# First two slabs behind a layer norm multiplied by input quarters, in a two-layer hybrid block on one core

## What is computed

```python
for l in range(DEPTH):                 # DEPTH = 2
    ...                                # proj = x @ w_in; main mixer; memory attention
    mixed = jnp.concatenate([main, mem_out], axis=-1) @ w_out[l]
    x = layer_norm(DEEPNORM_ALPHA * x + mixed, ln_g[l, 0], ln_b[l, 0])
    ffn = peer_ffn(x, peer_wq[l], peer_subkeys[l], peer_u[l], peer_v[l])
    x = layer_norm(DEEPNORM_ALPHA * x + ffn, ln_g[l, 1], ln_b[l, 1])
```

## Time and profile before

| | us |
|---|---|
| median of 3 runs | 3369.53 |
| lowest and highest of them | 3367.92 and 3376.97 |
| profiled execution | 3374.42 |
| its span, first to last instruction | 3372.6 |
| TensorE busy in it | 3321.4 |
| VectorE, ScalarE busy | 2779.2, 1925.3 |

### The profile page before, as it was taken

One profiled execution on the slowest core, in us unless ns is written; L12 is line 12 of the kernel. 1 busy time (PEld: TensorE's weight loads), 2 busy tenths in 40 slices (PEclk: granted clock), 3 DMA queues, 4 the chain that ended last, 5 costly groups with the idle time before them and its releaser, 6 DMA issues.

```text
span 3372.6 us, 51763 instructions
## 1 busy us (share of the span) xinstructions
PE 3321.4 (98%) x19516; PEld 2994.8 (89%) x19516; DVE 2779.2 (82%) x3848; ACT 1925.3 (57%) x3368; POOL 487.6 (14%) x264
## 2 busy tenths in 40 slices
PE   8999999999999999999999999999999999999998
PEld 7888879999999988887887887999999998888887
DVE  4664669998999978888986756999899988888897
ACT  5555545555666655555555545555666665555555
POOL 0000000011222211222310000011122221212330
PEclk9999999999999999999999999999999999999999
DMA  7554345797999989999984344578799988999995
GB/s 256 176 182 142 113 157 189 260 348 276 366 364 361 358 317 357 357 360 364 367 322 149 119 154 148 202 288 336 286 365 359 363 337 338 358 361 367 378 379 216
DMA packets 169074, 969.04 MB, mean 287 GB/s; under 512 B 18897, under 2 KB 52689, under 8 KB 55377
## 3 DMA queue, kind: packets, MB, share of 16 engines
q1 hardware_dynamic: 132048, 698.61, 55.6%
q0 software_dynamic: 36864, 268.45, 21.0%
HBM read 951.26 MB, written 15.73 MB: 287 GB/s over the span
## 4 chain that ended last, share of the span: by engine, by line
PE 91%; DVE 5%; DMA 2%; ACT 1%; issue 1%; SPq 0%; DVEq 0%; ACTq 0%
PE ps L943 90%; DVE wl L1577 1%; DMA raw<-in_v 1%; DMA arena<-in_v,idx 1%; PE ps L1133 1%; ACT wh L536 0%; DVE arena L1736 0%; DVE xx L1595 0%; DVE arena L1912 0%; DMA raw<-in_w 0%; DVE arena L1702 0%; DMA raw<-in_u 0%; ACT arena L595 0%; DVE arena L1680 0%; DVE arena L1683 0%
## 5 line engine op out<-in xcount | busy, mean ns | idle before, releaser
L1577 DVE TENSOR_TENSOR wl<-raw,wh 128x1024 fp32r<-128x1024 f32 x1264 | 1527.4, 1221 | 475.8 <-ACT wh L536 472.0
L943 PE MATMUL ps<-xx,wh 128*128 128x384 f32 (+1 forms) x5504 | 1710.2, 372 | 16.5 <-DVE wl L1577 11.5
L536 ACT ACTIVATE wh<-raw 128x1024 fp32r<-128x1024 f32 x1264 | 1334.9, 1057 | 618.9 <-PE ps L943 550.6
L943 PE MATMUL ps<-xx,wl 128*128 128x192 f32 (+1 forms) x5504 | 1422.0, 258 | 0.0
L943 PE MATMUL ps<-wh,act 128*128 128x512 f32 x3584 | 1190.7, 390 | 7.4 <-DVE act L1600 7.3
L943 PEld LDWEIGHTS ps<-xx,wh 128*128 128x128 f32 x5504 | 1034.4, 188 | 79.5 <-DVE wl L1577 11.8
L943 PEld LDWEIGHTS ps<-xx,wl 128*128 128x128 f32 x5504 | 1049.6, 191 | 0.5
L943 PE MATMUL ps<-wl,act 128*128 128x512 f32 x2304 | 897.1, 389 | 0.0
L943 PEld LDWEIGHTS ps<-wh,act 128*128 128x128 f32 x3584 | 673.4, 188 | 149.9 <-DVE wl L1577 6.7
L943 PEld LDWEIGHTS ps<-wl,act 128*128 128x128 f32 x2304 | 432.9, 188 | 89.6
L1548 POOL DMA_INDIRECT arena<-in_v,idx x128 | 272.4, 2128 | 834.1 <-DVE arena L1912 814.4
(11 more groups left out here) (213 smaller groups left out, 1698.3 us busy)
## 6 DMA issues: line engine op xcount, KB each, us to landing
raw<-in_u SPq DMA_DIRECT2D x256, 1024.0 KB
raw<-in_v SPq DMA_DIRECT2D x256, 1024.0 KB
raw<-in_w SPq DMA_DIRECT2D x119, 1024.0 KB
h_scratch<-hring SPq DMA_DIRECT2D x128, 96.0 KB
hring<-h_scratch SPq DMA_DIRECT2D x128, 96.0 KB
arena<-in_memT SPq DMA_DIRECT2D x4, 512.0 KB, 6.6
arena<-in_xT SPq DMA_DIRECT2D x4, 512.0 KB, 7.6
arena<-in_urows,idx POOLq DMA_INDIRECT x128
```

The lines of the kernel that those rows point to most:

```text
L536: nc.scalar.activation(wh[:, j, :], raw_piece(p), ACT.Copy).then_inc(hi_ready, 1)
L943: return nc.tensor.matmul(out, lhs, rhs, start=start, stop=stop, **kw)
L1577: v.tensor_tensor(wl[:, j, :], raw_piece(p), wh[:, j, :].bitcast(F32), ALU.subtract).then_inc(lo_ready, 1)
```

## The change

It touches the four norms and what stands directly before and behind them.

1. The first two slabs behind norms 0, 1 and 2 are multiplied together by a new function, `first_pair`: quarter 0 for slab 0 and slab 1, then quarter 1 for both, and so on. Quarters 0 to 2 are turned first; quarter 3 is turned after slab 0's share of quarter 0.
2. So the first halves of both slabs are needed before their second halves. `half_of` gives the new order: pieces p0, p0+1 are the first halves of slabs 0 and 1, p0+2 and p0+3 the second halves. The same order holds for the last two slabs of the N and V stages. In these, ScalarE makes the high part of each activation right behind one piece, not two, with a wait on `piece_used` of its own.
3. The norm centres four parts of 512 columns and goes by quarters: `turn(n, q)` turns banks q and 4 + q. Both engines finish quarter 0 (turned, high, low) before they start on quarter 1. Four pieces of the next stage are split inside the norm (AHEAD is gone, RING takes its place).
4. The side copy of slab 0 waits for one piece more (`split_by`), and the scores of heads 0 and 1 both stand in slab 2.

The core of the diff:

```diff
+def half_of(p):
+    for p0 in PAIRED_FIRST + PAIRED_LAST:
+        if p0 <= p < p0 + RING:
+            return p0 // 2 + (p - p0) % 2, (p - p0) // 2
+    return p // 2, p % 2
+
+def split_by(n):
+    return 2 * n + 2 + (2 * n in PAIRED_FIRST + PAIRED_LAST)
...
@@ SyncE
-                sp.wait_ge(lo_ready, 2 * (n - RAW_SLABS) + 2)
+                sp.wait_ge(lo_ready, split_by(n - RAW_SLABS))
@@ ScalarE, take_side
-            act.wait_ge(piece_used, k * 2 + (p0 + 2))
+            act.wait_ge(piece_used, split_by(p0 // 2) if k == 0 else k * 2 + (p0 + 2))
...
@@ ScalarE, norm
+            for q in range(3):
+                centred(q)
+            turned(0)
+            if n < 3:
+                high(0)
+            centred(3)
+            turned(1)
+            if n < 3:
+                high(1)
+            turned(2)
+            if n < 3:
+                high(2)
+                hi(p_next + 2, 2)
+                hi(p_next + 3, 3)
+            turned(3)
+            if n < 3:
+                high(3)
...
@@ ScalarE, v_trip
+                paired = i == S_EXP // 2 - 1
                 for s in range(2):
-                    for e in range(2):
-                        hi(i * RING + (v0 + 2 * s + e), 2 * s + e)
+                    for j in (s,) if paired else (2 * s, 2 * s + 1):
+                        hi(i * RING + v0 + j, j)
+                    if paired:
+                        act.wait_ge(piece_used, i * RING + v0 - 2 + 2 * s)
...
+                for j in (2, 3) if paired else ():
+                    hi(i * RING + v0 + j, j)
@@ TensorE
+        def first_pair(n, p0, t0, x_from):
+            for q in range(3):
+                turn(n, q)
+            pe.wait_ge(evac_done, t0)
+            for q in range(QX):
+                for s in range(2):
+                    j = q // 2 * 2 + s
+                    pe.wait_ge(lo_ready, p0 + j + 1)
+                    if s == 0:
+                        pe.wait_ge(x_ready, x_from + q + 1)
+                    if q == 0 and s == 1:
+                        turn(n, 3)
+                        pe.wait_ge(xta_ready, 8 * n + 4)
+                    side = ps[:, s, TOK:]
+                    both = ps[:, s, :].rearrange("p (a b) -> p a b", a=2)
+                    for k in range(CQ):
+                        kc = q * CQ + k
+                        if q == QX - 1 and s == 1 and k == CQ - 1:
+                            fold(t0, 0)
+                        w_hi, w_lo = (w[:, j, kc % (KC // 2) * P:(kc % (KC // 2) + 1) * P] for w in (wh, wl))
+                        mm(both, w_hi, xx[:, kc, :, :], kc == 0, False, skip_group_check=True)
+                        last = mm(side, w_lo, xh[:, kc, :], False, kc == KC - 1, skip_group_check=True)
+                    if q % 2:
+                        last.then_inc(piece_used, 1)
...
@@ TensorE, last_slabs_n and last_slabs_v
-            pe.wait_ge(lo_ready, piece + 3)
+            pe.wait_ge(lo_ready, piece + 2)
...
@@ VectorE, norm
+            for q in range(3):
+                centred(q)
+            turned(0)
+            centred(3)
             if n < 3:
-                low_quarter(xt, n + 2, QX - 1)
+                low_quarter(xt, n + 2, 0)
+            if n == 1:
+                lo(p_next + 1, 1)
+            turned(1)
+            if n < 3:
+                low_quarter(xt, n + 2, 1)
+            turned(2)
+            if n < 3:
+                low_quarter(xt, n + 2, 2)
                 lo(p_next + 2, 2)
+                lo(p_next + 3, 3)
+            turned(3)
+            if n < 3:
+                low_quarter(xt, n + 2, 3)
```

More of the change, by code:

```diff
@@ L645, in norm, with turned @@
[L645 to L648 removed]
+            def turned(q):
+                act.wait_ge(xtr_ready, 8 * n + 2 * q + 1)
+                for c in (4 * q, 4 * q + 1):
                     gain, shift = C_LN + 2 * n * KC + c, C_LN + (2 * n + 1) * KC + c
[L650 removed]
+                    nc.scalar.activation(xt[:, c, :], ps[:, q, (c % 2) * TOK:(c % 2 + 1) * TOK], ACT.Identity,
@@ L1212, in queries @@
         def queries(layer, p0, t0, x_count):
-            for k in range(S_WQ):
+            first_pair(2 * layer, p0, t0, QX * (x_count - 1))
+            for k in range(2, S_WQ):
                 def then(e, k=k):
-                    if e and k:
-                        scores(layer, k - 1, t0)
-                slab_t(p0 + 2 * k, t0 + k, k % 2, k, x_from=QX * (x_count - 1) if k == 0 else None, then=then,
-                       lone=k == 0)
+                    if e or k == 2:
+                        scores(layer, k - 2 + e, t0)
+                slab_t(p0 + 2 * k, t0 + k, k % 2, k, then=then)
         def experts(layer, u0, v0, t0):
@@ L1491, in group_scores @@
                 swa_scores(g - 2, bank)
-        for k in range(S_INB):
+        first_pair(1, P_INB, T_INB, 3 * QX)
+        for k in range(2, S_INB):
             g = k - SLAB_GROUP
@@ L1536, in _ @@
         n_stage(2, P_OUT1, S_OUT + S_EXP, S_OUT, then=inject_outs)
-        to_dims(2)
         queries(1, P_WQ1, T_WQ1, 5)
         experts(1, P_U1, P_V1, T_U1)
-        to_dims(3)
+        for q in range(QX):
+            turn(3, q)
     @block.gpsimd
@@ L1577, in lo @@
             v.tensor_tensor(wl[:, j, :], raw_piece(p), wh[:, j, :].bitcast(F32), ALU.subtract).then_inc(lo_ready, 1)
-        def ahead(p0):
-            for n in range(AHEAD):
-                lo(p0 + n, n)
         def split_t(p0, n, done=0):
@@ L1674, in norm @@
                     t, q = k // 2, 2 * half + k % 2
+                    if n < 3 and half and k == 1:
+                        lo(p_next + 1, 1)
                     summed(4 * half + k)
```

130 lines of the change are left out of this document (66 added, 64 removed).

## The result

The changed kernel took **3377.62 us** (median of 20 runs, 3373.69 to 3384.98); the kernel before, in 20 runs beside them, 3370.96. The ratio is 1.002, 95% interval 1.0014 to 1.0026: some 6.7 us slower, 0.2%, which is within the bound of 0.3%. The forecast was + 6.4 us (3375.9 from a median before of 3369.5).

A forecast was written before the change was run, and what follows sets the result against it. TensorE, busy 98% of the span, was taken as the bound, so changes pay only where it waits. Terms +2.0, +3.6, +1.7 and -0.9 sum to +6.4 us on the 3369.5 median: 3375.9 us, range 3367 to 3383.

The forecast's parts named there:

- Quarter 0, 1.1 us sooner: First seam: TensorE starts quarter 0's products at 471.85 instead of 472.98, a gain of 1.1 us.
- The relay, 3.3 us a quarter: VectorE and ScalarE hand each quarter over without overlap: 3.3 us a quarter, where high parts now come 2.00 apart.
- TensorE in the pair: First two slabs together: 2.8 us work a quarter, quarter 3 waits 1.6 us, end at 487.0; earlier start given back.
- The third slab, 1.45 us: Before slab 2, TensorE waits 1.45 us for piece 4's low half, split behind slab 0's later side copy.
- The seams: Stretches around the four norms: +2.0 us first, +3.6 second, +1.7 third, -0.9 last norm.
- the last norm: Norm with no piece following: first sum gains 0.6 us, one transpose wait of about 0.3 goes; -0.9.
- The additional term of the second seam: Behind norm 1, piece 1's low half also stands in the relay, between low 0 and turned 1: 1.13 us.
- The hidden relay: Rival: quarters arrive before TensorE asks for them; 3364 to 3368.5 us, chance 0.10.
- The late landing: Rival: slab 3's transfer, issued behind the subkeys, lands late; two more microseconds give +4, 3380 us; chance 0.10.
- The low clock: Rival: quarters 0 to 2 run at 1.2 GHz; 6 us in a seam, 3382 with one such seam; chance 0.10.
- That nothing changes: Rival: quarter 0 is no earlier, the relay slower by less, losses and gains cancel; 3369 to 3371 us, chance 0.08.
- if the clock falls inside the pair: Sign that the forecast is wrong: TensorE's clock falls while the first two slabs are multiplied together.

The follow-up runs named there:

- e6: Kernel before, with VectorE writing the low part of each quarter right behind its own slices of that quarter: 3387.33 us, ratio 1.0042.
- e9: As e6, but the low half of piece 1 stands between VectorE's slices and low part of quarter 1: 3379.26 us, ratio 1.0033.
- e4: Kernel before, with only the new order of the last two slabs of the out and V stages and their pieces: 3371.84 us, ratio 1.0000.
- e2: Changed kernel, with ScalarE making the high half of piece 4 ahead of slab 0's side copy: 3376.41 us, ratio 1.0015.
- e5: As e3, plus the high half of piece 4 ahead of slab 0's side copy: 3367.93 us, ratio 0.9986.
- e1: Changed kernel, with VectorE's slices of quarter q+1 ahead of the low part of quarter q: 3368.04 us, ratio 0.9989.
- e8: As e1, plus piece 4's high half ahead of slab 0's side copy, and slabs 3 and 4 issued ahead of the subkeys: 3368.44 us, ratio 0.9988.
- e7: As e5, plus SyncE issuing slabs 3 and 4 ahead of its wait for the four quarters and the subkeys: 3366.41 us, ratio 0.9986.
- e3: Changed kernel, with pieces 2 and 3 (second seam: 1 and 2) split where VectorE and ScalarE wait for each other: 3368.87 us, ratio 0.9994.
- e10: As e8 without the early issue of slabs 3 and 4: 3363.8 us, ratio 0.998.

## Why the prediction was right

**Quarter 0, 1.1 us sooner.** From the start of TensorE's wait to the first product it is 7.92 us after in the first and the third seam (461.70 to 469.62) and 9.64 and 9.83 before: 1.7 and 1.9 us. In the second, compared as above, about 0.6 us. The chain of quarter 0 was reckoned too long: low quarter 0 was forecast at 6.15 us after the centring began (465.6 to 471.75), and was written 5.57 us after (463.91 to 469.48). The step that was mis-sized is the transposes: they were taken at 0.20 us each, as at 1.2 GHz, so that VectorE's slices wait for the second half of quarter 0. In the first seam the granted clock was 1.00 until 469.5 and they didn't wait. In the second it was 0.50 from the first transpose on, VectorE waited 0.75 us for them, and low quarter 0 was written 6.40 us after the centring began, close to the forecast.

**The relay, 3.3 us a quarter.** Measured 3.31 and 3.33. Quarter 3 was forecast 18.4 us after the centring began and came after 17.80, in the third seam 17.80 as well (2051.42 to 2069.22). These are the same 0.6 us, carried on from quarter 0; the steps between were right. This and the kernels e6 and e9 are the core of the result. The relay put into the kernel before costs 11 us (e9; 14 in e6, with a low half in it). Taken out of the changed kernel it gives back 6.3 us by the seams. So the pair, with twice the work for each quarter, hides a part of it, yet not all; how large a part the intervals don't tell.

**TensorE in the pair.** Quarter 2 late by its weights: 1.31 and 1.01 us in the second and third seam, none in the first, where the low clock had stretched quarter 0. Quarter 3 late by 1.6: measured 1.08, 1.50, 1.47. The pair's end was forecast 21.4 us after the centring began and measured 21.1 (485.03).

**The third slab, 1.45 us.** 1.24, 1.26 and 1.25, for the reason given.

**The seams.** Forecast + 2.0, + 3.6, + 1.7, - 0.9; measured + 1.3, + 3.9, + 1.15, - 0.8. The sum of 6.4 is nearer to the medians' 6.66 than to the seams' 5.55, and that closeness is luck: two of the terms were too large, by 0.7 and 0.55 us, and one 0.3 too small. In the last norm 0.6 us were to come from the order of the last two slabs and 0.3 from centring by quarters; e4, which has the first alone, comes within 0.05 us of the changed kernel (23.83 and 23.78), so the second term isn't there. The additional term of the second seam, 1.13 us for piece 1 in the relay, is shown by e6 against e9. At its V stage the 0.88 us wait for an activation is gone and was worth nothing, as was said: the wait for the centred rows went from 5.54 to 7.15 us, and the first sum of norm 1 starts 2.95 us after the first-half products of slab 126, against 2.54 before (+ 0.45 was forecast).

**Rivals.** The hidden relay fell with e6 and with the waits for quarter 3. The late landing was half right: the wait of ScalarE for slab 3 was there (3.78 us), but cost nothing in the changed kernel and 0.4 us in one seam of e2. Its price had too little room: slab 3's first piece was to be ready 0.15 us before TensorE wants it, and was written 1.1 us before (492.46, slab 3 at 493.60), since quarter 3 came 0.6 us sooner and the high half began 8.4 us after it, not 9. What e2 paid for was not that piece but the copy-out behind the transfer, which the prediction didn't name. The low clock did not stay: quarter 0 alone was stretched, in the first seam. That nothing changes is out by the interval (4.7 to 8.8 us). The middle of the first rival's 3364 to 3368.5, from which the range starts, is 3366 and not 3367; nothing hangs on it.

**One sentence was wrong.** The prediction was to be wrong "if the clock falls inside the pair". It did, in the first seam, and the end of the relay was the same as in the third (17.80 us in both). The text above it had said why: TensorE is not what the pair waits for.

## What to carry to other kernels

Where two engines hand a thing back and forth, as here, look at the order within each: if the engine that starts an item also finishes it, start the next item before finishing this one, or put independent work where it would wait. A kernel that lets two slabs share each arriving quarter gains only if whatever prepared the third slab no longer stands behind the first two; follow the instruction that will be late next, in its queue, before counting the gain. And ask of a wait for a transfer what stands behind it on its engine and when that is wanted: 3.80 us of it cost nothing in e5, 4.25 us cost 0.41 in e2.

## What the runs showed of the hardware

**Where the clock falls is not fixed.** Stretches of the first seam after (us: span, then busy us of PE, PEld, DVE, ACT, POOL, then the granted clock, DMA share, GB/s):

```profile
466.00:468.00 2.00, 1.70 (x16) 1.47 (x14) 1.78 (x4) 1.91 (x4) 0.00 (x0) 1.00 0.03 8
470.00:472.00 2.00, 2.00 (x8) 1.65 (x7) 0.82 (x2) 1.53 (x3) 0.00 (x0) 0.50 0.00 0
```

Before, the granted clock was down from 465.64 to 472.47, through nearly all transposes. After, it stayed at 2.4 GHz through the first 24 (2.84 us, against 4.31 in the third seam, where it fell within them) and stood at 1.2 GHz from 469.75 to 473.2, in quarter 0. The waits of 1.0 to 1.5 us in the pair, which the prediction's third rival feared, left it at 2.4 GHz; the second seam shows it:

```profile
1789.00:1791.00 2.00, 0.69 (x5) 0.46 (x4) 2.00 (x3) 1.85 (x4) 0.00 (x0) 1.00 0.00 0
```

By the rule of the Trainium skill ("TensorE: Matmul & The Clock Gate", section "HAM oscillation — how this bites in real kernels") bursts parted by waits can each start at the low clock; for waits as short as these, this trace doesn't show it.

**The spread of the runs goes with the mean granted clock.** Of the 35 runs of the kernel before beside e1 to e4, those with a mean of 0.997 took 3368.4 us on average, 0.996: 3370.4, 0.995: 3374.3, 0.994: 3377.1. After: 3374.2, 3376.6, 3379.3, 3382.8. At the same clock the changed kernel is 5.0 to 6.2 us slower, about the seams' sum. In the runs beside e5 to e8, 0.996 and 0.997 both took 3369.6, so the steps are not even. In the profiles a large part of the spread comes from one place that the change doesn't touch. From a wait of 0.25 us at about 366 us on, the granted clock is 0.50 for some 13.7 us in the profiles of e2, e6, e7 and e8. In those of the kernel before, e1, e3 and e4 it is so for 3.4 us between 366 and 375 us, and in those of the changed kernel, e5, e9 and e10 it stays at 1.00. First e8, then e10:

```profile
360.00:380.00 20.00, 19.75 (x109) 17.40 (x104) 11.64 (x25) 8.26 (x18) 0.00 (x0) 0.66 0.21 77
360.00:380.00 20.00, 19.75 (x151) 17.50 (x146) 14.04 (x29) 9.75 (x20) 0.00 (x0) 1.00 0.24 89
```

e8 reaches its first seam 6.5 us later than e10 (467.60 and 461.13), in a span that is 8.7 us longer. What lowers the clock there in one run and not in the next stays open. Single stalls move between executions as well: TensorE waits 3.63 us for an activation near 1526 us in the profile before and 3.01 us near 3162 us after, at places that the change doesn't touch.
